# Down products with 512 moving columns per rounded weight load, in a 20-matrix float32 block on one core

## The reference

```python
def swiglu(h, w_gu, w_down):
    gate, up = jnp.split(h @ w_gu, 2, axis=-1)
    return (jax.nn.silu(gate) * up) @ w_down
...
x = x + 0.5 * swiglu(rmsnorm(x, ffn2_norm[layer]), ffn2_w_gu[layer], ffn2_w_down[layer])
```

## Time and profile before

| | |
|---|---|
| time, median of 2 runs | 1614.4 us (1614.24 to 1614.57) |
| profiled execution | 1607.0 us, span 1605.0 us |
| TensorE matmul / weight load busy | 96% / 92% of the span |
| VectorE / ScalarE / GpSimd busy | 66% / 46% / 4% |
| DMA engines, mean | 152 GB/s |
| granted TensorE clock, mean | 0.989 of 2.4 GHz |

### The profile page before, as it was taken

How to read it: one execution, slowest core, us unless ns; L and a number is a source line. 1 busy time by engine, 2 the same in 40 slices (tenths; PEclk the granted TensorE clock), 3 DMA queues, 4 the chain that set the end, 5 groups by cost and what they waited for, 6 DMA issues and landing times. The chain is left out here.

```text
span 1605.0 us, 36127 instructions
## 1 busy us (share of the span) xinstructions
PE 1536.2 (96%) x15669; PEld 1478.2 (92%) x15669; DVE 1064.6 (66%) x1277; ACT 730.3 (46%) x814; POOL 69.9 (4%) x52
## 2 busy tenths in 40 slices
PE   7999989999999999999998999999997889999998
PEld 6999989878999999999988999999886778999997
DVE  5766487764867547664677766467768776777436
ACT  5443345543534344433446433354565444555333
POOL 2000000100100001000101000021000000100000
PEclk9999999999999999999999999999999999999999
DMA  8665545201556556555533555564320012555552
GB/s 269 189 192 201 185 157 169 96 2 51 183 188 193 200 184 184 183 184 187 181 131 96 182 187 191 185 201 145 120 79 3 3 56 81 184 184 189 202 186 79
DMA packets 155065, 243.26 MB, mean 152 GB/s; under 512 B 9283, under 2 KB 106174, under 8 KB 154814
## 3 DMA queue, kind: packets, MB, share of 16 engines
q1 hardware_dynamic: 154510, 240.63, 45.7%
q10 hardware_dynamic: 432, 0.79, 0.2%
HBM read 240.34 MB, written 1.05 MB: 150 GB/s over the span
## 5 line engine op out<-in xcount | busy, mean ns | idle before, releaser
L2888 DVE TENSOR_TENSOR w_lo<-raw,w_hi 128x2048 fp32r<-128x2048 f32 x225 | 522.9, 2335 | 243.0 <-ACT w_hi L2715 242.1
L2518 PE MATMUL dense_ps<-h_hi,w_hi 128*128 128x256 f32 x2368 | 668.3, 282 | 12.2 <-DVE h_lo L2963 8.6
L2519 PE MATMUL dense_ps<-h_lo,w_hi 128*128 128x256 f32 x2368 | 662.0, 280 | 0.0
L2520 PE MATMUL dense_ps<-h_hi,w_lo 128*128 128x256 f32 x2368 | 662.0, 280 | 0.0
L2715 ACT ACTIVATE w_hi<-raw 128x2048 fp32r<-128x2048 f32 x225 | 428.5, 1913 | 332.6 <-DMA raw<-in_ffn_w_down 116.2
L2518 PEld LDWEIGHTS dense_ps<-h_hi,w_hi 128*128 128x128 f32 x2368 | 450.5, 190 | 18.3 <-issue 17.8
L2519 PEld LDWEIGHTS dense_ps<-h_lo,w_hi 128*128 128x128 f32 x2368 | 447.4, 189 | 0.8 <-issue 0.5
L2520 PEld LDWEIGHTS dense_ps<-h_hi,w_lo 128*128 128x128 f32 x2368 | 448.1, 189 | 0.0
L2520 PE MATMUL dense_ps<-g_hi,w_lo 128*128 128x256 f32 x960 | 266.9, 278 | 0.0
L2518 PE MATMUL dense_ps<-g_hi,w_hi 128*128 128x256 f32 x960 | 266.9, 278 | 0.0
L2519 PE MATMUL dense_ps<-g_lo,w_hi 128*128 128x256 f32 x960 | 266.9, 278 | 0.0
(11 more groups left out here) (554 smaller groups left out, 1750.5 us busy)
## 6 DMA issues: line engine op xcount, KB each, us to landing
raw<-in_ffn_w_gu SPq DMA_DIRECT2D x176, 512.0 KB, 4.6
raw<-in_ffn_w_down SPq DMA_DIRECT2D x88, 512.0 KB, 4.1
raw<-in_w_ff SPq DMA_DIRECT2D x64, 512.0 KB, 4.2
raw<-in_w_in SPq DMA_DIRECT2D x36, 512.0 KB, 4.4
raw<-in_a_w_in SPq DMA_DIRECT2D x32, 512.0 KB, 4.3
raw<-in_a_w_out SPq DMA_DIRECT2D x8, 512.0 KB, 4.0
raw<-in_b_w_in SPq DMA_DIRECT2D x8, 512.0 KB, 4.2
raw<-in_b_w_out SPq DMA_DIRECT2D x8, 512.0 KB, 4.1
```

Source lines behind the costliest of these rows:

```text
L2518: pe.matmul(o, hi, mh, start=start, stop=False)
L2519: pe.matmul(o, hi, ml, start=False, stop=False)
L2520: return pe.matmul(o, lo, mh, start=False, stop=stop)
L2888: dve.tensor_tensor(w_lo[:, p % SLOTS, :], raw[:, p % SLOTS, :], w_hi[:, p % SLOTS, :].bitcast(F32), ALU.subtract).then_inc(lo_ready, 1)
```

## The change

Three down products (of ffn1, ffn2 and ffn3) get a function of their own, `wide_two`. `g_hi` and `g_lo` become two halves of one tile, and a matmul with hi weights streams 512 columns, 256 of hi and 256 of lo activations, into a whole bank: columns 0 to 255 of the bank collect hi x hi, 256 to 511 hi x lo. The lo weights follow with 256 columns into the first half. So a triple becomes two matmuls and two loads, and 8 output tiles take all 8 banks, `D_ps` and `M_ps`. The last of the 11 pieces keeps three matmuls of 256 columns, all into the first halves, since VectorE adds the second halves to `xT` meanwhile: two more VectorE instructions per product, one when the first four output tiles are through the last but one piece, one when that piece is done. A new semaphore `low_kept` holds TensorE before each half of the last piece until they are done. The first piece takes the `M_ps` tiles first, the last but one the `D_ps` tiles first. ffn0 and ffn4 keep `wide`. 64 bytes are left free in front of `h_hi`, which moves every tile behind it by 64 bytes. In the hybrid stage the zeroing of `s_bd` moves ahead of the two copies, and `r_init` stands in for `r_zero`.

```diff
+    fixed.at += 64
     h_at = fixed.at
     h_hi = fixed.take("h_hi", [P, KD, T], F32R)
...
-    g_hi = m.take("g_hi", [P, NF, T], F32R)
-    g_lo = m.take("g_lo", [P, NF, T], F32R)
+    g_two = m.take("g_two", [P, 2, NF, T], F32R)
+    g_hi, g_lo = g_two[:, 0, :, :], g_two[:, 1, :, :]
...
+    TWO_HALVES = tuple(jobs_of[s_][1] for s_ in ("ffn1", "ffn2", "ffn3"))
+    def halves_of(job):
+        upto = wide_jobs[:wide_jobs.index(job) + 1]
+        return len(upto) + sum(j in TWO_HALVES for j in upto)
...
+        pool.memset(s_bd[:, :, :], 0.0)
         pool.tensor_copy(x_r[:, :, :], over_mid(ident, 8))
         pool.tensor_copy(xt_r[:, :, :], over_mid(ident, 8)).then_inc(r_init, 1)
-        pool.memset(s_bd[:, :, :], 0.0).then_inc(r_zero, 1)
...
+            def wide_two(job, two, ready):
+                p0, f0, n = PIECE_OF[job], FILL_OF[job], COUNT_OF[job]
+                def bank(nt):
+                    return (D_ps if nt < 4 else M_ps)[:, nt % 4, :]
+                for r in range(n):
+                    p = p0 + r
+                    pe.wait_ge(lo_ready, p + 1)
+                    pe.wait_ge(ready[0], ready[1](r))
+                    final = r == n - 1
+                    order = [(k, nt) for k in range(2) for nt in range(8)]
+                    if r == 0:
+                        order = [(k, nt) for e in (1, 0) for k in range(2) for nt in range(4 * e, 4 * e + 4)]
+                    if r == n - 2:
+                        order = [(k, nt) for e in (0, 1) for k in range(2) for nt in range(4 * e, 4 * e + 4)]
+                    if final:
+                        order = [(k, nt) for nt in range(8) for k in range(2)]
+                    for at_, (k, nt) in enumerate(order):
+                        kt = 2 * r + k
+                        if final and at_ % 8 == 0:
+                            pe.wait_ge(low_kept, 2 * TWO_HALVES.index(job) + at_ // 8 + 1)
+                        if r == 0 and at_ == 0:
+                            pe.wait_ge(dense_drained, f0 + 1)
+                        if r == 0 and at_ == 8:
+                            pe.wait_ge(dense_drained, f0 + 2)
...
+                        if final:
+                            for w, a in ((hi, 0), (hi, 1), (lo, 0)):
+                                last = pe.matmul(bank(nt)[:, 0:T], w, two[:, a, kt, :], start=False,
+                                                 stop=k == 1 and w is lo, skip_group_check=True)
+                        else:
+                            if kt:
+                                pe.matmul(bank(nt)[:, 0:T], lo, two[:, 0, kt, :], start=False, stop=False)
+                            last = pe.matmul(bank(nt).rearrange("p (a t) -> p a t", t=T), hi, two[:, :, kt, :],
+                                             start=kt == 0, stop=kt == 2 * n - 3)
+                            if kt == 0:
+                                last = pe.matmul(bank(nt)[:, 0:T], lo, two[:, 0, kt, :], start=False, stop=False)
+                        if r >= n - 2 and k == 1 and nt == 3:
+                            last.then_inc(half_filled, 1)
+                    last.then_inc(piece_used, 1)
...
             def residual(job, scale):
                 f0 = FILL_OF[job]
+                if job in TWO_HALVES:
+                    for e in range(2):
+                        if e == 0:
+                            dve.wait_ge(half_filled, halves_of(job) - 1)
+                        else:
+                            dve.wait_ge(piece_used, PIECE_OF[job] + pieces_of[job] - 1)
+                        x4 = xT[:, 4 * e:4 * e + 4, :]
+                        dve.scalar_tensor_tensor(out=x4, in0=(D_ps, M_ps)[e][:, :, T:2 * T], scalar=scale, in1=x4,
+                                                        op0=ALU.mult, op1=ALU.add).then_inc(low_kept, 1)
+                    dve.wait_ge(low_kept, 2 * TWO_HALVES.index(job) + 2)
```

More of the change, by code:

```diff
@@ L278, in build @@
     half_filled = sem("half_filled")
+    low_kept = sem("low_kept")
     dense_drained = sem("dense_drained")
@@ L354, in h_before @@
         return 4 * (NORM[stage] - (NORM[stage] > NORM["hybrid"]))
+    TWO_HALVES = tuple(jobs_of[s_][1] for s_ in ("ffn1", "ffn2", "ffn3"))
+    def halves_of(job):
+        upto = wide_jobs[:wide_jobs.index(job) + 1]
+        return len(upto) + sum(j in TWO_HALVES for j in upto)
     def wait_half(eng, job, e):
         if e == 0:
-            eng.wait_ge(half_filled, wide_jobs.index(job) + 1)
+            eng.wait_ge(half_filled, halves_of(job))
         else:
@@ L1541, in build @@
         "sum", "shift", "rank", "lora", "lsig", "g"))
-    r_free, r_dec, r_init, r_zero = sem("r_free"), sem("r_dec"), sem("r_init"), sem("r_zero")
+    r_free, r_dec, r_init = sem("r_free"), sem("r_dec"), sem("r_init")
     r_sqk, r_ssk, r_ssm, r_rk, r_kd, r_pq, r_ex, r_ops = (sem(f"r_{n}") for n in (
@@ L2277, in apply @@
             if i == 0:
-                dve.wait_ge(r_zero, 1)
+                dve.wait_ge(r_init, 2)
             whole = small_r[:, 32:40].rearrange("p (d i) -> p d i", d=2)[:, :, i]
@@ L2609, in wide @@
                     beside(2 * r + 1)
+            def wide_two(job, two, ready):
[22 more added lines that the diff above has]
+                            pe.wait_ge(dense_drained, f0 + 2)
+                        w0 = 1024 * k + P * nt
+                        hi, lo = w_hi[:, p % SLOTS, w0:w0 + P], w_lo[:, p % SLOTS, w0:w0 + P]
+                        if final:
[12 more added lines that the diff above has]
+                    last.then_inc(piece_used, 1)
@@ L2654, in _ @@
                     run_narrow(up, after_two=rest_turned if s == "ffn0" else lambda: None)
-                    wide(down, g_hi, g_lo, (g_ready, lambda r: chunk_of[up] + r + 1), halves=True)
+                    ready = (g_ready, lambda r: chunk_of[up] + r + 1)
+                    if down in TWO_HALVES:
+                        wide_two(down, g_two, ready)
+                    else:
+                        wide(down, g_hi, g_lo, ready, halves=True)
                 elif s == "mixer_a":
@@ L3004, in residual @@
                     wait_half(dve, job, e)
-                    x2 = xT[:, 4 * e:4 * e + 4, :].rearrange("p k t -> p (k t)")
-                    dve.scalar_tensor_tensor(out=x2, in0=D_ps[:, pair:pair + 2, :].rearrange("p a n -> p (a n)"),
-                                             scalar=scale, in1=x2, op0=ALU.mult, op1=ALU.add).then_inc(dense_drained, 1)
+                    if job in TWO_HALVES:
+                        x2, product = xT[:, 4 * e:4 * e + 4, :], (D_ps, M_ps)[e][:, :, 0:T]
+                    else:
+                        x2 = xT[:, 4 * e:4 * e + 4, :].rearrange("p k t -> p (k t)")
+                        product = D_ps[:, pair:pair + 2, :].rearrange("p a n -> p (a n)")
+                    dve.scalar_tensor_tensor(out=x2, in0=product, scalar=scale, in1=x2, op0=ALU.mult,
+                                             op1=ALU.add).then_inc(dense_drained, 1)
                     if e and next_stage(stage_of[job]) in ("mixer_a", "ple"):
```

## The result

The changed kernel takes 1647.3 us (1647.0 and 1647.6) against 1614.4 us: 1.021 of the time before, 95% interval 1.0145 to 1.0275. The profiled executions went from a span of 1605.0 to 1644.9 us, 39.9 us more. The forecast was 1608 us.

What follows compares the result with a forecast made beforehand. TensorE's own matmul stream was taken as the bound. Terms -1.0 + 1.5 - 7.0 = -6.5 us on the profiled 1607.0 gave 1600.5, plus 7.4 for unprofiled runs: 1608 us; eight in ten between 1575 and 1630.

Steps and rivals of the forecast that it cites:

- The 64 bytes: Shift of the activation tiles: pitch bounded between 109.4 and 120.0 ns, effect on the time taken as nothing.
- the rival: Equal remainders of weight and activation addresses to 128 collide in every stage: 120.0 ns, 58 us more, 1672 us; chance 0.10.
- The 512 columns: Merged matmuls in three down products: 480 triples each save 2.1 ns on average, 1.0 us in all, at best 9.4.
- Loads bind: Rival for TensorE: loads set the pitch, so fewer loads save 9.4 us; 1606.5 us, or 1599 with a changed stretch; chance 0.15.
- The additions and the wait: TensorE waits for VectorE before the last piece: 0.5 us lost in ffn1, 1.0 in ffn2, none in ffn3; sum 1.5.
- Hidden work: `h_hi` wait, residual reads, load order and the hybrid stage's earlier `s_bd` zeroing (0.31 us) were to cost nothing.
- Which pitch: Pitches of ffn1 to ffn3 and what follows drawn anew: one long stretch turns short, -7.0 us, between -14.1 and +7.0.

Runs made afterwards that it cites:

- experiment 2: Kernel before plus only the 64 free bytes in front of the activations: 1653.2 us, 1.033 of before.
- experiment 3: Changed kernel with 128 free bytes instead of 64 (distance 64): 1627.8 us, 1.018 of before.
- 5 to 8: Changed kernel with 192, 256, 320 and 384 free bytes instead of 64, in this order: 1637.9, 1612.7, 1644.7 and 1627.0 us.
- experiment 1: Changed kernel without the 64 free bytes: 1604.8 us, 1.0013 of before.
- experiments 4 and 13: 4: changed kernel, 64 bytes in front of everything, weights too: 1603.1 us. 13: changed kernel, 64 bytes behind `h_lo` instead of in front of `h_hi`: 1619.4 us.
- 9 and 10: Kernel before with one kind of weights at distance 0, the other at 192: lo weights at 0 in 9, 1635.5 us; hi weights in 10, 1635.6 us.
- experiment 14: Changed kernel without the 64 free bytes, keeping banks, order and waits, but three matmuls of 256 columns instead of the merged pair: 1607.3 us, 0.998 of before.

## Why the prediction was wrong

**The 64 bytes: the step that failed.** The prediction bounded them by 109.4 and 120.0 ns and took nothing, since two pitches occur with the same addresses. The reason does not hold: that two pitches occur at one distance, 192, does not keep another distance from having others, and distance 0 has 120.0 ns alone. Taking nothing for this term left out 48 us of loss (below), against a forecast gain of 6.5. The measured value is the upper bound to the last digit, 120.0 ns, read off the gate logits. That was the only row whose operands stood at the changed kernel's distance (`h_hi` and `ba_hi`, both 64 past a multiple of 256), and an unknown price between far ends should have gone to that row, which was nearest. Instead the rival had 0.10, and its 1672 us stood outside the range. The prediction also concluded from the 16-byte lines of the Trainium skill ("SBUF — State Buffer", on cachelines) that the shift does nothing; experiment 2 refutes the conclusion. Whether the lines are of that size no run here shows.

**The rival's size.** It counted 1056 long triples in 3600. In fact nearly half of these matmuls were long (mixers, hybrid and the small products too): 1800 x 20.0 + 1800 x 6.7 = 48 us, less 6.4 for merged pairs, plus the wait, gives 42 us; the spans differ by 39.9. Its extent, every stage from the first up product on, is what the trace shows; that reads get in each other's way is not shown. That the remainder to 128 counts was too coarse: experiment 3 rules it out, and 5 to 8 fit 256.

**The 512 columns.** Predicted were 2.1 ns less than a triple for a pair, so 337.9 ns behind a short and 351.2 behind a long pitch, 1.0 us saved in all. At the old distance it is 353.3 in every product, so the merging saves nothing there against the long pitch and costs up to 480 x 13.3 = 6.4 us against the short one. Line 1171 gave the length of a 512-column matmul rightly (388 to 398 ns), but in two of a kind, from which the pitch of alternating shapes could not be had. In the changed kernel, at distance 0, the pair gains 13.3 ns on the triple. "Loads bind" is refuted as well: with one load fewer, a pair took 346.7 to 353.3 ns where that rival had 329.3, and the 512-column matmuls had 392 to 398 ns (medians by product) where it had 379.

**The additions and the wait.** 1.5 us predicted, 0.2 measured in ffn1, none in ffn2 and ffn3. VectorE's split came earlier against the last piece: its end is 1.1, 1.6 and 1.6 us ahead of it in ffn1, ffn2 and ffn3. Hidden work was hidden: `h_hi`, the gaps between stages and GpSimd's order cost nothing visible.

**Which pitch.** The prediction called this its largest certain term, 7.0 us less. The draw is real at distance 192, but nothing of it is in this result: at distance 0 there is one pitch, and the two runs are 0.6 us apart. Nor does a draw favour the change: without the 64 bytes (experiment 1) the time is that of before.

**What stays open.** Why the distance matters in steps of 64 and less, with a period of 256, is not shown. Reads of weights and columns that get in each other's way would fit experiments 4 and 13. The finer form of that, that only the matmul over a bad load suffers, fails in nearly all of 9 and 10, and fits five short stretches of 9. Nor is it shown what picks 113.3 or 117.8 ns after a stop, why the short one turns up in short stretches at distance 64, or why alternating 512 and 256 columns always took 353.3 ns at distance 192, and 346.7 or 353.3 at distance 0.

## What to carry to other kernels

Look at the start-to-start pitch of back-to-back matmuls before moving a buffer, and compare it after: an address shift of 64 bytes can change every fp32r product of a program by 2 to 6%. Where a kernel has such a pitch at its best, keep the distance between stationary and moving operands modulo 256 when adding tiles, and test edits of layout and of computation apart. And a price for which the trace has a row with the same configuration is that row's price, even if the row is a side product of 24 matmuls.

## What the hardware showed that I had not expected

- Back-to-back fp32r matmuls of 256 columns with a load each, at a granted clock of 1.00, have pitches of 113.3, 117.8 and 120.0 ns at distances 192 and 0, constant through whole products of 60 to 120 us (others, from 117.2 ns, at distances between); 113.3 held through a feed-forward stage only at distance 192.
- At distance 0 the loads are longer too: 192 ns in the changed kernel, against 188 at distance 192 with the short pitch. At distance 64 they have 187 to 188 ns, and the pitch is long all the same.
- At one distance the pitch can survive a change of product: ffn3's up product and down product in experiment 14 both have 276 ns. In the traces of before and of experiments 1, 4, 6 and 14 it changed only where two starts lay 0.27 us or more apart or where matmuls of another shape or operand pair (the norm's, the mixers', the 512-column ones) came between.
- The same program varied by 19 to 26 us from run to run, by the traces mostly through that draw; the kernels with a constant pitch varied by 3 us or less.
